# Attention scores as three single-pass products of split queries and keys

## What is computed

```
q, k, v = jnp.split(h @ w_in, [DA_QK, 2 * DA_QK], axis=-1)   # 16 maps of 64 for q and k, 8 heads of 128 for v
for blk in range(S // BLOCK):                                  # 4 blocks of 128 queries
    s = jnp.einsum('bmqd,bmkd->bmqk', q[:, :, qs:ke], k[:, :, :ke]).astype(jnp.float32)
    s = jnp.where(rel >= 0, s + bias, -jnp.inf)
    a = jax.nn.softmax(s, axis=-1).reshape(B, H, 2, BLOCK, ke)
    a = a[:, :, 0] - lam_full * a[:, :, 1]
    outs.append(jnp.einsum('bhqk,bhkv->bhqv', a.astype(v.dtype), v[:, :, :ke]))
o = rms_norm(o, subln) * (1.0 - lam_init)
return o @ w_out
```

## Time and profile before

| | |
|---|---|
| median of 3 runs | 3608.49 us |
| lowest and highest | 3605.56 and 3609.68 us |
| span of the profiled execution | 3604.3 us, 44631 instructions |
| PEld busy | 2976.9 us (83%) |
| DVE busy | 1754.0 us (49%) |
| ACT busy | 937.0 us (26%) |
| POOL busy | 656.0 us (18%) |
| mean granted TensorE clock | 0.997 |

### The profile page before, as it was taken

The page is one execution under the profiler, slowest core; times in us unless marked ns, Lnnn a source line. Parts: engine busy times, 40 slices in busy tenths (PEclk is TensorE's granted clock), DMA queues, the critical chain, the costliest instruction groups (busy, mean ns, idle before and its releaser), DMA issues.

```text
span 3604.3 us, 44631 instructions
## 1 busy us (share of the span) xinstructions
PE 3542.8 (98%) x18618; PEld 2976.9 (83%) x18618; DVE 1754.0 (49%) x2185; ACT 937.0 (26%) x1658; POOL 656.0 (18%) x382
## 2 busy tenths in 40 slices
PE   8999999999999999999999999999999999999999
PEld 6778888888888888688888877888888888898887
DVE  4455334546563336563335445543464346564434
ACT  2552001312230013541003256310141214220102
POOL 2113111211031112121112110311121111211110
PEclk9999999999999999999999999999999999999999
DMA  5312222211122222212222222222222222322222
GB/s 205 106 71 94 94 94 94 94 71 59 47 101 94 94 95 103 74 67 104 94 94 94 100 77 77 97 94 94 94 71 94 75 91 84 114 99 101 94 94 71
DMA packets 57282, 329.60 MB, mean 91 GB/s; under 512 B 5580, under 2 KB 12236, under 8 KB 20349
## 3 DMA queue, kind: packets, MB, share of 16 engines
q1 hardware_dynamic: 44604, 303.79, 23.5%
q10 hardware_dynamic: 12480, 22.96, 1.9%
HBM read 323.96 MB, written 8.80 MB: 92 GB/s over the span
## 4 chain that ended last, share of the span: by engine, by line
PE 86%; DVE 7%; ACT 5%; issue 1%; POOL 1%; DMA 1%; DVEq 0%; ACTq 0%; POOLq 0%
PE proj L490 23%; PE proj L492 22%; PE proj L491 22%; PE proj L611 2%; PE proj L612 2%; PE proj L613 2%; PE proj L523 2%; PE proj L524 1%; PE proj L525 1%; DVE wlo L1709 1%; PE mix L791 1%; PE mix L685 1%; DVE s L1817 1%; ACT h L1169 1%; ACT xh L1166 1%
## 5 line engine op out<-in xcount | busy, mean ns | idle before, releaser
L463 POOL TENSOR_SCALAR whi<-raw 128x2048 fp32r<-128x2048 f32 x286 | 555.9, 1944 | 2720.2 <-DVE wlo L1709 1684.1
L490 PE MATMUL proj<-gh,whi 128*128 128x512 f32 x1968 | 785.0, 399 | 12.7 <-ACT gh L1118 10.5
L492 PE MATMUL proj<-gh,wlo 128*128 128x512 f32 x1968 | 770.2, 391 | 0.0
L491 PE MATMUL proj<-gl,whi 128*128 128x512 f32 x1968 | 769.6, 391 | 0.0
L1709 DVE TENSOR_TENSOR wlo<-raw,whi 128x2048 fp32r<-128x2048 f32 x286 | 653.3, 2284 | 136.5 <-POOL whi L463 118.4
L490 PE MATMUL proj<-xh,whi 128*128 128x512 f32 x1760 | 696.0, 395 | 8.6 <-DVE wlo L1709 2.8
L491 PE MATMUL proj<-xl,whi 128*128 128x512 f32 x1760 | 689.1, 392 | 0.0
L492 PE MATMUL proj<-xh,wlo 128*128 128x512 f32 x1760 | 688.9, 391 | 0.0
L490 PEld LDWEIGHTS proj<-gh,whi 128*128 128x128 f32 x1968 | 370.4, 188 | 106.4 <-issue 15.8
L492 PEld LDWEIGHTS proj<-gh,wlo 128*128 128x128 f32 x1968 | 370.3, 188 | 80.9
L491 PEld LDWEIGHTS proj<-gl,whi 128*128 128x128 f32 x1968 | 370.5, 188 | 78.7 <-issue 2.2
(11 more groups left out here) (303 smaller groups left out, 4300.0 us busy)
## 6 DMA issues: line engine op xcount, KB each, us to landing
raw<-in_stream SPq DMA_DIRECT2D x286, 1024.0 KB, 4.8
da_b<-bias_da ACTq DMA_DIRECT2D x16, 512.0 KB, 3.4
bias_da<-bias_rows ACTq DMA_DIRECT2D x8, 512.0 KB, 9.0
h<-in_x ACTq DMA_DIRECT2D x4, 512.0 KB, 8.9
bias_sw<-bias_table ACTq DMA_DIRECT2D x1, 2048.0 KB, 10.0
pf<-in_p ACTq DMA_DIRECT2D x4, 512.0 KB, 6.9
sw_b<-bias_sw ACTq DMA_DIRECT2D x4, 512.0 KB, 3.8
out_features<-fin SPq DMA_DIRECT2D x8, 256.0 KB, 2.5
```

The lines of the kernel that those rows point to most:

```text
L463: nc.gpsimd.tensor_scalar(whi[SLOT[n]][:, :, :], raw[SLOT[n]][:, :, :], 1.0, 0.0, ALU.mult, ALU.add).then_inc(hi_done, 1)
L490: nc.tensor.matmul(out, wh, ah, start=first, stop=False, skip_group_check=check)
L491: nc.tensor.matmul(out, wh, al, start=False, stop=False, skip_group_check=check)
L492: return nc.tensor.matmul(out, wl, ah, start=False, stop=last, skip_group_check=check)
```

## The change

The release of the queries' and keys' units in the two attention mixers goes from ACT to DVE. `da_q` and `da_k` become F32R, so ACT's copy leaves the rounded part. A new step on DVE, `score_lo`, takes the rest from the same PSUM banks (full minus rounded), into blocks of `xl` for the queries and of `xh` for the keys: blocks 4 and 5 for even groups, 6 and 7 for odd ones. The scores become three products for each of the two maps: rounded by rounded, rounded queries by the keys' rest, the queries' rest by rounded keys. On ACT the copies of queries and keys move ahead of second(k - 1) and exps(k); that of the values stays behind them. On DVE `score_lo` stands behind mask(k) and ahead of coef(k - 1); for the first group it stands between the splits of slabs.

```diff
@@ -78,7 +78,7 @@
     for layer in range(NL):
         kind, j = layer % 3, layer // 3
         if kind == 0:
-            pl.stage(f"mix{layer}", [("da_w_in", j, 0, c + g * 256) for g in range(4) for c in (0, D, 2 * D)], ["act"])
+            pl.stage(f"mix{layer}", [("da_w_in", j, 0, c + g * 256) for g in range(4) for c in (0, D, 2 * D)], ["dve", "dve", "act"])
             out = ("da_w_out", j)
         elif kind == 1:
             pl.stage(f"mix{layer}", [("hg_w_in", 0, 0, c + g * 256) for g in range(4) for c in (D, 0, 2 * D, 3 * D)], ["act"])
@@ -278,8 +278,8 @@
         sg = Arena(sg_at)("sg", [P, 2, 2, S])
 
         a = Arena()
-        da_q = a("da_q", [P, 2, 2, S])
-        da_k = a("da_k", [P, 2, 2, S])
+        da_q = a("da_q", [P, 2, 2, S], F32R)
+        da_k = a("da_k", [P, 2, 2, S], F32R)
         da_v = a("da_v", [P, 2, 4, 256])
         da_b = a("da_b", [P, 2, 2, S])
         da_s = a("da_s", [P, 2, 2, S])
@@ -390,7 +390,7 @@
                 m[name] = sem(name)
             return m[name]
 
-        for name in ("start_pe start_act start_dve relu_done half_done h_half h_gate sg_half s1_added sq_done s2_added stats var_done "
+        for name in ("start_pe start_act start_dve da_hi relu_done half_done h_half h_gate sg_half s1_added sq_done s2_added stats var_done "
                      "std_done norm_ready spread ln_u ln_full low_even half_x half_r r_hi p_in p_hi p_lo h_new scores masked negmax expd coef second "
                      "attn transposed at_copied av o_sq o_ms o_std o_rstd o_norm z_done "
                      "hg_prod hg_sc hg_pick hg_far_copied hg_keys hg_std hg_rstd hg_normed hg_turned kdup kcopy rot_in rot_mm rot_done decay_in "
@@ -680,10 +680,14 @@
                         pe.wait_ge(rel[e], v)
                     if it:
                         pe.wait_ge(M("masked"), 2 * it)
-                    for mp in range(2):
-                        r = slice(64 * mp, 64 * mp + 64)
-                        last = nc.tensor.matmul(mix[:, mp, 0:(qb + 1) * P], da_q[r, g % 2, hh, qb * P:(qb + 1) * P],
-                                                da_k[r, g % 2, hh, 0:(qb + 1) * P], start=True, stop=True)
+                    qc, kc = slice(qb * P, (qb + 1) * P), slice(0, (qb + 1) * P)
+                    hl = 4 + 2 * (g % 2) + hh
+                    for i in range(3):
+                        for mp in range(2):
+                            r = slice(64 * mp, 64 * mp + 64)
+                            q_ = xl[r, hl, qc] if i == 2 else da_q[r, g % 2, hh, qc]
+                            k_ = xh[r, hl, kc] if i == 1 else da_k[r, g % 2, hh, kc]
+                            last = nc.tensor.matmul(mix[:, mp, kc], q_, k_, start=i == 0, stop=i == 2)
                     last.then_inc(M("scores"), 1)
 
                 def transposes(k):
@@ -1214,7 +1218,7 @@
                         ins = A(da_k[:, g % 2], banks(u), ACT.Copy)
                     else:
                         ins = A(da_v[:, g % 2].rearrange("p (b s) n -> p b (s n)", b=2), banks(u), ACT.Copy)
-                    ins.then_inc(*own.sig(rel["act"]))
+                    ins.then_inc(*own.sig(rel["act"] if j == 2 else M("da_hi")))
 
                 def exps(k):
                     it, qb = 32 * d + k, k % 4
@@ -1254,15 +1258,17 @@
                 for k in range(32 + 5):
                     if layer == 0 and k == 18:
                         act.dma_start(bias_sw, bass.AP(tensor=table.tensor, offset=640 + 383, ap=[[1280, 16], [-1, P], [1, 256]])).then_inc(biased_sw, 16)
+                    i = DA_FILLED.index(k - 1) if k - 1 in DA_FILLED else -1
+                    if i >= 0 and i % 3 < 2:
+                        evac(i // 3 + 1, i % 3)
                     if 1 <= k < 33:
                         second(k - 1)
                     if k < 32:
                         exps(k)
                         if k % 4 == 3 and k // 4 + 2 < 8:
                             bias_in(k // 4 + 2)
-                    if k - 1 in DA_FILLED:
-                        i = DA_FILLED.index(k - 1)
-                        evac(i // 3 + 1, i % 3)
+                    if i >= 0 and i % 3 == 2:
+                        evac(i // 3 + 1, 2)
                     if k >= 7 and k % 4 == 3:
                         head_hi((k - 7) // 4)
                     if 2 <= k < 34:
@@ -1992,11 +1998,30 @@
                     V.scalar_tensor_tensor(xl[:, hd, :], post_on[:, :], small[:, 10 + d:11 + d], xh[:, hd, :].bitcast(F32), ALU.mult, ALU.subtract)\
                         .then_inc(*own.sig(xl_ready if hd % 2 else M("six_lo") if hd == 6 else None))
 
+                def score_lo(g, j):
+
+                    u = u0 + 3 * g + j
+                    dve.wait_ge(M("da_hi"), 8 * d + 2 * g + j + 1)
+                    if g >= 2:
+                        dve.wait_ge(M("scores"), 32 * d + 8 * (g - 1))
+                    pair_ = slice(4 + 2 * (g % 2), 6 + 2 * (g % 2))
+                    full = banks(u)
+                    if j == 0:
+                        ins = V.scalar_tensor_tensor(xl[:, pair_, :], full, -0.125, da_q[:, g % 2].bitcast(F32), ALU.mult, ALU.subtract)
+                    else:
+                        ins = V.tensor_tensor(xh[:, pair_, :], full, da_k[:, g % 2].bitcast(F32), ALU.subtract)
+                    ins.then_inc(*own.sig(rel["dve"]))
+
                 for j in range(3):
                     low_parts(s0 + j + 3)
+                    if j < 2:
+                        score_lo(0, j)
                 for k in range(32 + 4):
                     if k < 32:
                         mask(k)
+                    if k - 1 in DA_FILLED and DA_FILLED.index(k - 1) % 3 < 2:
+                        i = DA_FILLED.index(k - 1)
+                        score_lo(i // 3 + 1, i % 3)
                     if 1 <= k < 33:
                         coef(k - 1)
                     if k >= 7 and k % 4 == 3:
```

## The result

The changed kernel takes 3613.1 us in the median of 21 runs (3609.0 to 3617.0), the kernel before in the same comparison 3606.7 (3604.0 to 3609.7, 21 runs). The ratio is 1.0017, with an interval of 1.0011 to 1.0024: +6.4 us. So it is slower, surely so, but by less than the 0.2% that I had set as the bound, and inside the range. The forecast stood at 3610.1, that is at +1.6 instead of +6.4. As a time it missed by 3.0 us only, because it was added to the 3608.5 us of three runs, which lie 1.8 above the median of 21: that part is luck. The profiled execution has a span of 3612.3 us against 3604.3.

The account below looks back on a forecast made before the run. TensorE, busy for 98% of a 3604.3 us span, was taken as the bound. Terms -4.5 + 0.8 + 3.2 + 0.7 + 1.4 = +1.6 us gave a 3605.9 span, 3610.1 as time; range 3600 to 3621.

Parts of the forecast that it names:

- The products: Scores in both attention mixers: three single passes instead of the fp32 product change the slots, -4.5 us in all.
- +0.8 given back: Ends of both mixers: what scores 29 to 31 save is lost to PE's waits there, +0.8 us.
- (A): Score products: the row halves don't run side by side in single-pass form; +31 us, 3639.5 us; chance 0.13.
- (B): Score products: weight load of the second and third isn't hidden behind the same half's stream; +11.3, 3619.8 us; chance 0.08.
- (C): Score products: a 128-wide single pass is as slow as the whole fp32 product; 5.9 more, 3616.0 us; chance 0.07.
- Iterations 15 and 23: In both mixers: a wait for `post_on` replaces the wait for the key copy, +0.8 us each, +3.2 us in all.
- (D): Iterations 15 and 23: `head_norm` doesn't hold the values back; -6.4 us in all, 3602.1 us; chance 0.06.
- The start of layer 0: Before unit 2: the bank comes free 1.22 us later, after `score_lo`; PE gets back 0.56; +0.7 us.
- The clock: Half clock follows the stall before values 12 in both layers, where one of two did before: one more, +1.4 us.
- four of them: Upper end of the range for half-clock drops in the mixers: four drops would cost +4.2 us.
- Nothing elsewhere: Iterations 3, 6, 12 and 20: moved copies and new rests cost nothing; without cover each up to 1.2 us.

Follow-up runs that it names:

- experiment 1: The run of `e1_norm_first`: `score_lo` moved behind `head_norm` on DVE, against the changed kernel; 3601.1 us.
- e5_halves_in_turn: The changed kernel with all three products of one half issued, then all three of the other: 3613.8 us, ratio 1.0017 to the kernel before.
- e6_stalls_filled: The changed kernel with repeated transposes filling PE's idle time ahead of values 12 and 20: 3606.0 us, ratio 0.9996 to the kernel before.
- e9_after_chunks: The changed kernel with two more chunks of the next projection by iteration 15 and one more by 23: 3597.4 us, ratio 0.9971 to the kernel before.
- e4_low_parts_only: The changed kernel with fp32 score products again and the rests formed but unread: 3616.2 us, ratio 1.0026 to the kernel before.
- e1_norm_first: The changed kernel with `score_lo` moved behind `head_norm` on DVE: 3601.1 us, ratio 0.9985 to the kernel before.
- e3_products_only: The kernel before with three single-pass score products on rounded parts, without rests: 3604.3 us, ratio 0.9994 to the kernel before.
- e2_copies_behind: `e1_norm_first` with the copies of queries and keys put back behind the exponentials: 3615.7 us, ratio 1.0023 to the kernel before.

## Why the prediction came out as it did

*The products* (-4.5, with +0.8 given back, so -3.7): measured -3.4, each slot within 0.02 us. For the steps of the table's first row alone the forecast comes to -4.1, against -3.6. Most of the difference is the step behind scores 27, where PE waited 0.73 us for `post_on` before and waits as long after (0.76 and 0.72): the shorter product saves nothing there, 0.16 in each layer, and the prediction had no term for it. Pairs start together, so (A) is out; a bare weight load would have made the 128-key slot 0.58, so (B) is out: here 64-row loads of the same half hide behind its stream (0.11 us from the second product's start to the third's, 53.20 to 53.31; and the 512-key slot is 0.90 where (B) has 1.06). The Trainium skill (TensorE: Matmul & The Clock Gate, The mechanism) has a load overlap a running matmul only where the row group differs, and beside it names a background weight buffer as a second way. The trace decides against the first as a rule without exception, and agrees with the second. (C) is out at 0.48 instead of 0.85.

*Iterations 15 and 23* (+3.2): 8.75, 8.75, 8.74 and 9.10, that is +3.5. The end of the chain was right to 0.02 us (its links came up to 0.13 sooner than written), and (D) is refuted by the wait for `post_on` and by experiment 1. The 9.10 I had not foreseen. In layer 3 DVE starts `post_on` later than its order explains (timeline of DVE, iteration 23):

```profile
2192.10 0.21 DVE L1983 TENSOR_SCALAR small<-small 128x1 f32<-128x1 f32 x1
2192.77 0.69 DVE L1957 TENSOR_TENSOR post_on<-mix,post_rs 128x512 f32<-128x512 f32 x1 [0.46 <-DVE small L1983]
```

In the three other places 0.1 us lies between the two. The same place is as long in `e5_halves_in_turn`, `e6_stalls_filled` and `e9_after_chunks` (9.10 or 9.11) and 0.35 longer than in layer 0 in `e4_low_parts_only` (9.22), but as long as in layer 0 in `e1_norm_first` (6.96). Why stays open.

*The start of layer 0* (+0.7): unit 2 waits 1.63 us for `xl` (41.37 against 40.18). The profile pair gives +1.1 at scores 1, but the copy before it starts anywhere from 37.86 to 39.11 us over the kernels, behind ACT's DMA issues. Eight profiles with the rests have scores 1 at 55.99 to 56.99 (mean 56.5), three without at 55.46 to 56.32 (mean 55.9): some 0.6, near the forecast, with a scatter as large, so it is not confirmed. The way there was not quite right either: the step from scores 0 to 1 went from 3.61 to 3.48 us, so in this pair PE got back 0.1 to 0.2 of the 0.56 that I had counted.

*The clock* (+1.4): this is the step that failed, +4.6 instead. The sentence was "I take a drop in both layers: one more". It counted only the stalls before values 12 as a risk. Those before values 20 had grown too, to 1.87 and 2.22 us of unbroken idle time against 1.09 before, and each of them was followed by the same 1.5 us. The forecast expected half clock after both stalls before values 12 and says nothing of the other two; the case "four of them" stood in the text, at its top end of +4.2, and was the right one. The mechanism was named and the count was off. With four stretches in the sum the forecast would have been 3613. That 1.87 us of idle time is enough for one could not be read off the trace of before, where the longest in the mixers was 1.77; what could be read is that the stalls before values 20 outgrow it.

*Nothing elsewhere*: right. There is no wait in iterations 3, 6, 12 or 20.

## What to carry to other kernels

Where an instruction that waits for another engine is put into a hand-written order, look at what is queued behind it for what is ready sooner: here one `post_on` of 0.69 us behind a rest that waited for its copy cost 12 us, and swapping the two was free. Count an idle stretch of TensorE twice, once for its length and once for the clock that may follow; filling it with work already at hand (three chunks moved) was worth more than the cheaper products. And follow each stall that the change lengthens by itself: the second one looked like the first and was left out of the clock's count.

## What I had not expected of the hardware

- Single-pass products on the two row halves run in pairs even if issued one half after the other: slots of 0.49 and 0.90 us at 128 and 512 keys in both orders.
- Idle stretches of 1.87, 2.22 and 3.25 us were all followed by half clock in the changed kernel, about 1.5 us lost each time; with 26 transposes in the place of the longest one, leaving 0.64 us, there was none. Shorter ones went either way: 0.46 and 1.77 us with values between dropped it in one layer of two before and in both in `e3_products_only`, 0.49 and 0.89 in one of two in `e1_norm_first`. So near there a small change elsewhere decides over 1.5 us.
- A stretch at half clock isn't always the same: after the 3.02 us of idle time in `e2_copies_behind` scores 16 to 17 took 7.94 and 7.96 us, 2.2 over their length at full clock, where 7.25 is usual. The half clock held for 6.8 us there and began while PE was still idle. After 3.2 us of idle time it was so once of two times in `e4_low_parts_only` (7.99) and in `e5_halves_in_turn` (7.96), but not in the changed kernel with its 3.25. So the length of the stall doesn't decide it, and the runs don't show what does.
